# A decoder block on one core: the first block's tail goes under the expert loop, and the block input is loaded as rows and turned by TensorE

## The chip, the core and the metric

The kernel runs as one program on one core of a Trainium2 chip. The core has TensorE (PE: matmuls, with its weight loads shown as PEld), VectorE (DVE), ScalarE (ACT), GpSimd (POOL) and SyncE (SP, which here only issues DMAs), each with its own instruction stream; they meet through semaphores. Sixteen DMA engines move data between HBM and the on-chip memories. The metric is device time in microseconds (us), lower is better.

## The reference, cut to what matters

```python
h = x
xn = rmsnorm(h, norm_mix_w)                       # x: (1, 1024 tokens, 1024 channels), float32
proj = xn @ w_in                                  # q/k/v for 8 stick-breaking heads, q/k/v/o/i/f for 4 mLSTM heads, 2 gates
mixed = (sigmoid(g_sb) * (y_sb @ w_branch_sb) + sigmoid(g_ml) * (y_ml @ w_branch_ml)) @ w_out
h = h + mixed
hn = rmsnorm(h, norm_ffn_w)
q  = (hn @ w_query).reshape(T, 8 heads, 2, 128)   # PEER: product keys
s1, s2 = q[:, :, 0] @ keys1, q[:, :, 1] @ keys2   # 128 scores each; top 16 of each, then top 16 of the 256 sums
e_idx, gate = ...                                 # 8 * 16 = 128 experts of 16384 per token, softmax gates
act = gelu(expert_u[e_idx] . hn)                  # per token 128 rows of u (1024 floats) and 128 rows of v
h = h + (gate * act) @ expert_v[e_idx]
out = rmsnorm(h, norm_final_w)
```

## The kernel before, in words

**Two kinds of work.** The 1024 tokens are 8 tiles of 128 (`TT = 8`); two tiles make a block of 256 tokens (`NB = 4` blocks). The mixer, from the first norm to the PEER scores, is done block by block by a generator `mix(b)` in every engine's stream. One `yield` ends one step; the steps come in sections: `N_NORM` steps of norm, 13 of first projections (`PROJ1`, one 512 KB weight unit each), the stick-breaking attention (SBA, from `n_sba(b)`), `PROJ2`, `N_MIX`, `N_OUT`, `N_HN` (norm of h, and hn turned for the query matmuls), and `N_QRY = 19` steps: `QRY` units 0 to 15 are query matmuls; in steps 4, 8, 12 and 16 PE also does the scores of one of four head groups, and one step later (5, 9, 13, 17) ACT copies them out.

The expert work is done per tile in 64 slots (`PP = 64`), a pair of experts in each. POOL gathers one expert row of u and v for each of the 128 tokens (L885, 1 MB per gather, `rowsb<-uv,e_idx`) into a ring of 8 buffers (`RS = 8`, so four pairs); DVE forms the dot product with the normed row `hnrow` (L1479); ACT applies gelu (`gelu`, L1070), the gate (L1080) and builds two diagonal matrices (`spread`, L1085); PE adds the v rows (`add_rows`, L819), which signals `v_done`. A gather waits for the `v_done` of the pair that had its buffer. Before a tile's gathers DVE must have picked the experts: `top_parts(i, g)` for each of four head groups (36 parts per tile), then `gates`. In tile 0 (i = 0) one part is done in each slot, for groups 1 to 3 of tile 0 and all of tile 1; in later tiles the 36 parts of the next tile lie in slots 24 to 59.

**The order.** On every engine, `mix(0)` runs to its end first; SP then loads `hnrow` of tile 0 (`load_hn(0)`, L517); DVE does `top_parts(0, 0)` and `gates(0, 0, 1)` before its first dot, ACT does its half of these gates (L1065) behind step 13 of N_QRY. Then the loop over tiles and slots starts, and blocks 1 to 3 lie under it: `steps[s][b]` says how many steps of block b are done in slot s. A planner spreads each block's steps over its slots (block 1: slots 0 to 99, block 2: 100 to 227, block 3: 228 to 355) so that the estimated cost of a step (`load_of`, 2.0 for a norm step) is even over the slots. In a slot PE does first `add_rows` and then the mixer steps, except in slot 0 of a tile.

**The norm of the block input.** x comes in transposed, from a second copy of x made by the host (`xT`), as 8 loads of 128 KB in runs of 1 KB (`load_x`, L426), channels on partitions. ACT squares each chunk of 128 channels (L913), PE sums over channels with a matmul by ones (L623), two chunks at a time because `sq` has two buffers; ACT takes the square root (L916), DVE the reciprocal over 128x256 (L1131), and DVE multiplies each chunk by weight and factor (L1135, 8 times). The loads for block b+1 are issued in odd steps of block b's N_QRY. All loads but the gathers go through SP's queue, which is in order.

Of the kernel before, what the change touches and what calls it, by code (L numbers as in the profile page):

```python
# [11 lines left out]
ALU = mybir.AluOpType  # L12
# [3 lines left out]
P = 128  # L16
# [49 lines left out]
def build(nc, xT, x, vecs, w_feat, w_if, w_tok, w_merge, w_out, w_query, keysT, uv, rows, out):  # L66
    ctx = ExitStack()
    with ctx:
# [62 lines left out]
        sq = cut(A_EXT, 2 * N).rearrange("p (u t) -> p u t", u=2)  # L131
        rstd = cut(A_EXT + 2 * N, N)
# [64 lines left out]
        x_loaded = [sem(f"x_loaded{k}") for k in range(KD)]  # L197
        sq_ready, sq_summed, xn_ready = sem("sq_ready"), sem("sq_summed"), sem("xn_ready")
# [63 lines left out]
        for b in range(NB):  # L262
            put(("ss", b), 0, 0)
# [68 lines left out]
        N_NORM, N_PROJ1, N_PROJ2 = 7, len(PROJ1) + 1, len(PROJ2) + 1  # L332
# [3 lines left out]
        def load_of(b):  # L336
            unit = 8 * N * 1.67e-3 + 0.2
            cost = [2.0] * 7
# [39 lines left out]
        with nc.Block() as block:  # L378

            @block.sync  # L380
            def _(sp):
# [54 lines left out]

                def mix(b):
                    t0 = NT * b
                    if b == 0:
                        for k in range(KD):  # L440
                            load_x(0, k)
# [52 lines left out]
                    for k in range(N_QRY):  # L494
# [8 lines left out]
                        if k % 2 == 1 and k // 2 < KD and b + 1 < NB:  # L503
                            load_x(b + 1, k // 2)
# [8 lines left out]
                def load_hn(i):  # L513
                    sp.wait_ge(hn_stored[i], 16)
                    if i > 1:
                        sp.wait_ge(dot_done, (i - 1) * NSEL)
                    sp.dma_start(hnrow[:, i % 2, :], hn_dram[i * P:(i + 1) * P, :]).then_inc(hn7_loaded[i % 2], 16)  # L517

# [4 lines left out]
                for _step in mix(0):  # L523
                    pass
                load_hn(0)
                later = [mix(b) for b in range(1, NB)]
                for i in range(TT):
                    for p in range(PP):
# [9 lines left out]
                        for b in range(1, NB):  # L538
                            for _n in range(steps[i * PP + p][b]):
                                next(later[b - 1], None)  # L540
# [6 lines left out]
            def _(pe):  # L547
# [66 lines left out]
                def mix(b):  # L614
                    t0 = NT * b

                    for k in range(N_NORM):
                        if k < 4:
                            if k == 0:
                                vacant(pe, ("ss", b))  # L620
                            for c in (2 * k, 2 * k + 1):
                                pe.wait_ge(sq_ready, b * KD + c + 1)
                                pe.matmul(X[:, 0, 0:N], ones[:, :], sq[:, c % 2, :], start=c == 0,  # L623
                                          stop=c == KD - 1).then_inc(sq_summed, 1)
                        yield
                    for k in range(N_PROJ1):
                        if k == 0:
                            pe.wait_ge(xn_ready, (b + 1) * KD)
# [195 lines left out]
                for _step in mix(0):  # L824
                    pass
                later = [mix(b) for b in range(1, NB)]
                for i in range(TT):
                    for p in range(PP):
                        if p > 0:
                            add_rows(i, p)  # L830
                        for b in range(1, NB):
                            for _n in range(steps[i * PP + p][b]):
                                next(later[b - 1], None)
                        if p == 0:
                            add_rows(i, p)
# [55 lines left out]
            def _(act):  # L891
# [13 lines left out]
                def mix(b):  # L905
                    t0 = NT * b
                    for k in range(N_NORM):
                        if k < 4:
                            for c in (2 * k, 2 * k + 1):
                                act.wait_ge(x_loaded[c], 16 * (b + 1))  # L910
                                if c >= 2:
                                    act.wait_ge(sq_summed, b * KD + c - 1)
                                act.activation(sq[:, c % 2, :], xn[:, c, :], ACT.Square).then_inc(sq_ready, 1)  # L913
                        if k == 4:
                            act.wait_ge(sq_summed, (b + 1) * KD)
                            act.activation(rstd, X[:, 0, 0:N], ACT.Sqrt, scale=1.0 / D, bias=eps[:, 0:1]).then_inc(x_taken[0], 1)  # L916
# [182 lines left out]
                later = [mix(b) for b in range(1, NB)]  # L1099
                for i in range(TT):  # L1100
                    for p in range(PP):
# [4 lines left out]
                        for b in range(1, NB):  # L1106
                            for _n in range(steps[i * PP + p][b]):
                                next(later[b - 1], None)
# [7 lines left out]
            def _(dve):  # L1116
# [9 lines left out]
                def mix(b):  # L1126
                    t0 = NT * b
                    for k in range(N_NORM):
                        if k == 5:
                            emptied(dve, ("ss", b))  # L1130
                            mark(dve.reciprocal(rstd, rstd))  # L1131
                            settle()
                        if k >= 5:
                            for c in range(4 * (k - 5), 4 * (k - 5) + 4):
# [450 lines left out]
```

## Time and profile before

| | |
|---|---|
| median of 3 runs | 3449.7 us (3446.57 to 3456.82) |
| the profiled execution | 3442.75 us |
| its span (first to last instruction) | 3440.6 us |
| PE / DVE / ACT / POOL busy | 77% / 63% / 31% / 34% |
| DMA | 1280.42 MB, mean 372 GB/s |

The page cuts the span in 40 slices of 86 us. A digit is the busy share in tenths; PEclk is the TensorE clock that was granted, in tenths of full speed; DMA is the mean busy share of the 16 DMA engines:

```profile
PE   7999687898888778887887878898787555555554
DVE  2322479776456787786447698776457755775444
PEclk8999899999998999999998989999998767777777
DMA  3335798999999999999999989999999999999997
```

The first gather is issued in the fourth slice; up to there the DMA engines are a third busy, and from the sixth on they are nearly full.

### The profile page before, as it was taken

How to read it: one execution, taken by the hardware profiler on the slowest of the kernel's cores; microseconds unless marked ns; L12 is line 12 of the kernel's file. 1: busy time of each engine (PE TensorE's matmuls, PEld its weight loads, DVE VectorE, ACT ScalarE, POOL GpSimd, SP SyncE). 2: the span in 40 equal slices, each digit the busy share in tenths (PEclk: the TensorE clock that was granted, in tenths of full speed). 3: DMA queues.
4: the chain of work that ended last, by engine and by line, in shares of the span. 5: the costliest groups of instructions: out<-in, count | busy, mean ns of one | idle time of the engine just before them, and what ended most of it. 6: DMA issues, size and time to landing. Idle time of an engine off the chain costs nothing.

```text
span 3440.6 us, 40277 instructions
## 1 busy us (share of the span) xinstructions
PE 2645.8 (77%) x14496; PEld 1346.8 (39%) x14496; DVE 2151.8 (63%) x4980; ACT 1067.3 (31%) x3378; POOL 1185.5 (34%) x1049
## 2 busy tenths in 40 slices
PE   7999687898888778887887878898787555555554
PEld 5676444455354334554353334454253111111111
DVE  2322479776456787786447698776457755775444
ACT  2111234333223363332223363332222232223222
POOL 0000233334323343333333344433233434443442
PEclk8999899999998999999998989999998767777777
DMA  3335798999999999999999989999999999999997
GB/s 111 104 120 188 290 417 322 362 416 414 399 402 406 413 356 411 418 418 406 410 414 411 415 313 406 417 419 417 417 394 419 421 415 421 421 418 407 421 421 317
DMA packets 229127, 1280.42 MB, mean 372 GB/s; under 512 B 25536, under 2 KB 29632, under 8 KB 97856
## 3 DMA queue, kind: packets, MB, share of 16 engines
q0 software_dynamic: 147456, 1073.81, 76.2%
q1 hardware_dynamic: 81472, 204.04, 16.2%
q8 instruction: 115, 1.88, 0.2%
q14 instruction: 84, 0.69, 0.1%
HBM read 1260.97 MB, written 16.78 MB: 371 GB/s over the span
## 4 chain that ended last, share of the span: by engine, by line
DMA 39%; PE 35%; DVE 13%; ACT 6%; issue 5%; POOL 3%; POOLq 0%; ACTq 0%; DVEq 0%; SPq 0%
DMA rowsb<-uv,e_idx 34%; PE yacc L819 13%; PE mixp L561 9%; DVE rowsb L1479 5%; PE mixp L586 4%; DMA wt<-w_query_ 3%; POOL rowsb L885 3%; PE mixp L610 2%; PE mixp L599 2%; DVE area L1152 2%; PE mixp L573 2%; ACT diag L1085 2%; ACT wg L1080 1%; ACT area L903 1%; ACT gmt L1070 1%
## 5 line engine op out<-in xcount | busy, mean ns | idle before, releaser
L885 POOL DMA_INDIRECT rowsb<-uv,e_idx x1024 | 1180.8, 1153 | 2223.9 <-PE yacc L819 1720.5
L1479 DVE CUSTOM_DVE_ANT_0 rowsb<-rowsb,hnrow 128x1024 f32<-128x1024 f32 x1024 | 1241.3, 1224 | 853.6 <-DMA rowsb<-uv,e_idx 830.7
L819 PE MATMUL yacc<-rowsb,diag 64*64 64x512 f32 x8192 | 1226.0, 724 | 658.5 <-ACT diag L1085 639.6
L819 PEld LDWEIGHTS yacc<-rowsb,diag 64*64 64x64 f32 x8192 | 301.0, 151 | 1411.7 <-ACT diag L1085 974.7
L1070 ACT ACTIVATE gmt<-dots 128x2 f32<-128x2 f32 x512 | 104.0, 203 | 1725.5 <-DVE dots L1479 1724.7
L561 PE MATMUL mixp<-area,wt 128*128 128x256 f32 x2304 | 538.7, 389 | 16.3 <-ACT area L903 10.0
L561 PEld LDWEIGHTS mixp<-area,wt 128*128 128x128 f32 x2304 | 434.7, 193 | 154.3 <-issue 91.5
L1085 ACT ACTIVATE diag<-ident,wg 128x64 f32<-128x64 f32 x1024 | 300.3, 340 | 16.7
L586 PE MATMUL mixp<-area,wt 128*128 128x256 f32 x1024 | 247.5, 399 | 37.7 <-DMA wt<-w_query_ 36.7
L903 ACT ACTIVATE area<-mixp 128x512 f32<-128x512 f32 (+3 forms) x384 | 162.8, 467 | 361.6 <-PE mixp L561 163.2
L1080 ACT ACTIVATE wg<-gmt,gate 128x1 f32<-128x1 f32 x1024 | 245.7, 286 | 17.4
L586 PEld LDWEIGHTS mixp<-area,wt 128*128 128x128 f32 x1024 | 199.0, 199 | 108.7 <-DMA wt<-w_query_ 48.9
L610 PE MATMUL mixp<-area,wt 128*128 128x256 f32 x512 | 119.4, 389 | 6.2 <-DMA wt<-w_merge 6.2
L599 PE MATMUL mixp<-wt,area 128*128 128x512 f32 x256 | 118.2, 609 | 3.4 <-DMA wt<-w_out_ 3.4
L573 PE MATMUL mixp<-wt,area 128*128 128x512 f32 x256 | 117.5, 606 | 1.4 <-DMA wt<-w_tok 1.4
L610 PEld LDWEIGHTS mixp<-area,wt 128*128 128x128 f32 x512 | 97.2, 194 | 34.7 <-issue 15.1
L1152 DVE TENSOR_TENSOR_SCAN area<-area 128x128 f32<-128x128 f32 (+7 forms) x64 | 86.9, 1358 | 2.2
L1479 DVE DVE_READ_ACCUMULATOR2_ANT dots<- 128x1 f32 x1024 | 84.2, 82 | 0.0
L599 PEld LDWEIGHTS mixp<-wt,area 128*128 128x128 f32 x256 | 47.3, 193 | 76.3 <-issue 74.6
L573 PEld LDWEIGHTS mixp<-wt,area 128*128 128x128 f32 x256 | 47.1, 191 | 71.9 <-issue 69.5
L643 PE MATMUL mixp<-keys_sb,area 64*128 64x512 f32 (+3 forms) x192 | 52.1, 590 | 10.3 <-ACT area L903 9.1
L654 PE MATMUL mixp<-ident,area 128*128 128x128 f32 x288 | 49.1, 309 | 10.7 <-DVE area L1154 10.5
(183 smaller groups left out, 1689.2 us busy)
## 6 DMA issues: line engine op xcount, KB each, us to landing
wt<-w_merge SPq DMA_DIRECT2D x96, 512.0 KB, 8.0
wt<-w_feat SPq DMA_DIRECT2D x80, 512.0 KB, 8.1
wt<-w_query_ SPq DMA_DIRECT2D x64, 512.0 KB, 12.1
wt<-w_tok SPq DMA_DIRECT2D x32, 512.0 KB, 10.4
wt<-w_out_ SPq DMA_DIRECT2D x32, 512.0 KB, 8.5
rowsb<-uv,e_idx POOLq DMA_INDIRECT x1024, 13.1
area<-xT SPq DMA_DIRECT2D x32, 128.0 KB, 13.6
area<-x_rows SPq DMA_DIRECT2D x4, 1024.0 KB, 17.9
```

Source lines behind the costliest of these rows:

```text
L561: last = pe.matmul(X[:, bank(key), at:at + N], w[:, c * P:(c + 1) * P], src[:, c, :], start=c == 0, stop=c == KD - 1)
L573: last = pe.matmul(X[:, bank(key), :], xn[:, 2 * n + c, t * P:(t + 1) * P], w[:, c * NCH:(c + 1) * NCH], start=n == 0 and c == 0, stop=n = ...
L586: last = pe.matmul(X[:, bank(key), at:at + N], w[:, c * NCH + f * P:c * NCH + (f + 1) * P], hnT[:, 2 * m + c, :], start=m == 0 and c == 0 ...
L599: last = pe.matmul(X[:, bank(key), :], mgT[:, n, t * P:(t + 1) * P], w[:, c * NCH:(c + 1) * NCH], start=n == 0, stop=n == KD - 1)
L610: last = pe.matmul(X[:, bank(key), f * N:(f + 1) * N], w[:, at:at + P], src[:, c, :], start=c == 0, stop=c == 3)
L819: last = pe.matmul(yacc[at:at + HP, r, c * NCH:(c + 1) * NCH], diag[r * HP:(r + 1) * HP, s, :], rowsb[r * HP:(r + 1) * HP, s, D + c * NCH: ...
L885: pool.indirect_dma_start(rowsb[:, n % RS, :], None, uv, bass.IndirectOffsetOnAxis(ap=e_idx[:, i % 2, k:k + 1], axis=0)).then_inc(row_load ...
L903: act.activation(to, src, fn, **kw).then_inc(x_taken[bank(key)], 1)
L1080: act.activation(wg[:, s:s + 1], gmt[:, s:s + 1], ACT.Copy, scale=gate[:, i % 2, k:k + 1]).then_inc(wg_done, 1)
L1085: last = act.activation(diag[:, s, :], ident7[:, :], ACT.Copy, scale=wg[:, s:s + 1])
L1152: mark(dve.tensor_tensor_scan(left[:, T - m:T][:, ::-1], back, back, 1.0, ALU.mult, ALU.min))
L1479: dve.tensor_tensor_reduce(rowsb[:, s, 0:D], rowsb[:, s, 0:D], hnrow[:, i % 2, :], 1.0, 0.0, ALU.mult, ALU.add, dots[:, s:s + 1]).then_inc ...
```

## The change

1. **Tail of block 0.** All engines run `mix(0)` only up to and with step 12 of N_QRY (`N_HEAD`, all but the last 6 steps). These last 6 steps (query units 13, 14, 15, the scores of the fourth group and the copies out) are done one per slot in slots 0 to 5 of tile 0. In slot 0 of tile 0 PE does `add_rows` ahead of the mixer step. Block 1 is spread over slots 3 to 99.
2. **Gates and hnrow of tile 0.** ACT does its half of the first gates ahead of step 12 of N_QRY. SP issues `load_hn(0)` in step 3 of block 0's N_QRY.
3. **Block input.** x is loaded as rows (tokens on partitions), 2 loads of 512 KB in runs of 4 KB, in steps 7 and 9 of N_QRY, into the place of `hn`. ACT squares a tile of 128x1024 with a sum along the row, twice, and takes the square root of 2 columns; DVE takes the reciprocal of 2 columns and makes two diagonal matrices `scale1` (128x128). PE multiplies each 128x128 piece of x by the diagonal, 16 matmuls, which turns and scales it; ACT copies 8 pieces of 128x256 out with the norm weight as scale. The section has 3 steps instead of 7, with planner costs 2.0, 4.5, 2.5. Norms of blocks 1 to 3 are done in the same new way.

```diff
-            put(("ss", b), 0, 0)
+            for c in range(4):
+                put(("xt", b, c), c)
-        N_NORM, N_PROJ1, N_PROJ2 = 7, len(PROJ1) + 1, len(PROJ2) + 1
+        N_NORM, N_PROJ1, N_PROJ2 = 3, len(PROJ1) + 1, len(PROJ2) + 1
-            cost = [2.0] * 7
+            cost = [2.0, 4.5, 2.5]
+        N_HEAD = len(cost[0]) - 6
+        for s in range(6):
+            steps[s][0] = 1
         for b in range(1, NB):
-            lo = 0 if b == 1 else NT * (b - 1) * PP - PP + BLOCK_END
+            lo = 3 if b == 1 else NT * (b - 1) * PP - PP + BLOCK_END
 # SP
-                def load_x(b, k):
-                    if b > 0 and k == 0:
+                def load_x(b, t):
+                    if b > 0 and t == 0:
                         for i in range(NT * (b - 1), NT * b):
-                            sp.wait_ge(h_stored[i], 16)
-                        sp.wait_ge(hn_ready, NT * b)
-                    sp.dma_start(xn[:, k, :], xT[k * P:(k + 1) * P, b * N:(b + 1) * N]).then_inc(x_loaded[k], 16)
+                            sp.wait_ge(hn_stored[i], 16)
+                        for n in range(NT):
+                            ready(sp, ("hT", b - 1, n, 1))
+                    sp.dma_start(xr[:, t, :], x[(NT * b + t) * P:(NT * b + t + 1) * P, :]).then_inc(x_loaded[t], 16)
-                        if k % 2 == 1 and k // 2 < KD and b + 1 < NB:
-                            load_x(b + 1, k // 2)
+                        if k == 3 and b == 0:
+                            load_hn(0)
+                        if k in (7, 9) and b + 1 < NB:
+                            load_x(b + 1, (k - 7) // 2)
 # PE, norm section
-                            for c in (2 * k, 2 * k + 1):
-                                pe.wait_ge(sq_ready, b * KD + c + 1)
-                                pe.matmul(X[:, 0, 0:N], ones[:, :], sq[:, c % 2, :], start=c == 0,
-                                          stop=c == KD - 1).then_inc(sq_summed, 1)
+                        if k == 1:
+                            pe.wait_ge(scale_ready, b + 1)
+                            for c in range(4):
+                                vacant(pe, ("xt", b, c))
+                                for f in range(2):
+                                    for t in range(NT):
+                                        at = f * N + t * P
+                                        last = pe.matmul(X[:, c, at:at + P], xr[:, t, (2 * c + f) * P:(2 * c + f + 1) * P],
+                                                         scale1[:, t, :], start=True, stop=True)
+                                last.then_inc(x_done[c], 1)
 # PE, main loop (SP, ACT and DVE alike: the steps of block 0 among those of the slots)
-                for _step in mix(0):
-                    pass
-                later = [mix(b) for b in range(1, NB)]
+                later = [mix(b) for b in range(NB)]
+                for _n in range(N_HEAD):
+                    next(later[0])
                 for i in range(TT):
                     for p in range(PP):
-                        if p > 0:
+                        if p > 0 or i == 0:
                             add_rows(i, p)
 # ACT, norm section
+                        if k == 0:
+                            for t in range(NT):
+                                act.wait_ge(x_loaded[t], 16 * (b + 1))
+                                act.activation(sq[:, t, :], xr[:, t, :], ACT.Square, accum_out=ssq[:, t:t + 1]).then_inc(xsq_ready, 1)
+                            act.wait_ge(xsq_ready, NT * (b + 1))
+                            act.activation(ssq[:, NT:2 * NT], ssq[:, 0:NT], ACT.Sqrt, scale=1.0 / D,
+                                           bias=eps[:, 0:1]).then_inc(xstd_ready, 1)
+                        if k == 2:
...
+                            for c in range(KD):
+                                key = ("xt", b, c // 2)
+                                ready(act, key)
+                                ins = act.activation(xn[:, c, :], X[:, bank(key), c % 2 * N:(c % 2 + 1) * N], ACT.Copy,
+                                                     scale=vec[:, V_NORM1 + c:V_NORM1 + c + 1])
...
 # ACT, head
-                for n, _step in enumerate(mix(0)):
-                    if n == len(cost[0]) - N_QRY + 13:
+                for n in range(N_HEAD):
+                    if n == len(cost[0]) - N_QRY + 12:
                         gates(0, 0, 1)
+                    next(later[0])
 # DVE, norm section
+                            dve.wait_ge(xstd_ready, b + 1)
+                            mark(dve.reciprocal(ssq[:, 0:NT], ssq[:, NT:2 * NT]))
                             settle()
+                            for t in range(NT):
+                                last = dve.tensor_scalar(scale1[:, t, :], ident[:, :], ssq[:, t:t + 1], None, ALU.mult)
+                            last.then_inc(scale_ready, 1)
```

## Rows read from the trace of the kernel before

**Rows 1.** Busy time by stretch: span, PE, PEld, DVE, ACT, POOL, PEclk, DMA share, GB/s.

```profile
341.00:364.00 23.00, 17.64 (x84) 15.19 (x83) 0.07 (x1) 2.42 (x5) 7.70 (x8) 0.93 0.97 372
364.00:384.00 20.00, 13.21 (x67) 10.91 (x65) 0.54 (x3) 5.10 (x9) 0.00 (x0) 1.00 0.74 266
384.00:399.00 15.00, 7.06 (x28) 3.25 (x32) 10.71 (x36) 5.15 (x17) 0.00 (x0) 0.66 0.16 54
399.00:436.00 37.00, 27.73 (x170) 14.14 (x163) 29.91 (x71) 13.13 (x41) 16.29 (x14) 0.91 0.92 362
700.00:1190.00 490.00, 416.32 (x2248) 229.36 (x2246) 303.91 (x741) 152.13 (x484) 172.27 (x153) 0.93 1.01 408
1190.00:1290.00 100.00, 75.02 (x577) 35.59 (x575) 87.90 (x125) 59.46 (x180) 47.97 (x34) 0.88 0.91 360
1975.00:2065.00 90.00, 71.08 (x530) 34.20 (x534) 84.78 (x107) 60.65 (x155) 38.62 (x27) 0.85 0.83 317
```

**Rows 2.** Who waited for whom from 341 to 400 us: total, times, longest.

```profile
POOL rowsb L885 <- PE yacc L819: 47.9, 1, 47.9
DVE gs L1464 <- ACT gate L1065: 25.4, 1, 25.4
DVE rowsb L1479 <- DMA hnrow<-hn_scratch: 20.6, 1, 20.6
```

**Rows 3.** POOL in order of time: the ninth gather and the 23rd.

```profile
399.06 0.93 POOL L885 DMA_INDIRECT rowsb<-uv,e_idx  x1 [47.87 <-PE yacc L819]
436.01 1.20 POOL L885 DMA_INDIRECT rowsb<-uv,e_idx  x1 [2.33 <-PE yacc L819]
```

**Rows 4.** PE in order of time: query unit 12, its scores, one slot later on.

```profile
357.22 5.29 PE L586 MATMUL mixp<-area,wt 128*128 128x256 f32 x16 [5.36 <-DMA wt<-w_query_]
362.34 1.95 PE L805 MATMUL mixp<-area 128*128 128x128 f32 x16
422.70 1.95 PE L819 MATMUL yacc<-rowsb,diag 64*64 64x512 f32 x16
424.58 3.72 PE L561 MATMUL mixp<-area,wt 128*128 128x256 f32 x16
```

**Rows 5.** ACT in order of time: the table load of the first gates.

```profile
364.94 1.28 ACT L1065 ACT_TABLE_LOAD   x1
```

**Rows 6.** The head in order of time, ACT and PE.

```profile
5.65 1.28 ACT L913 ACT_TABLE_LOAD   x1 [5.65 <-POOL ident L875]
20.29 30.66 PE L561 MATMUL mixp<-area,wt 128*128 128x256 f32 x128 [6.26 <-DVE area L1135]
30.26 0.60 ACT L903 ACTIVATE keys_sb<-mixp 128x512 f32<-128x512 f32 x1 [15.20 <-PE mixp L561]
37.17 0.60 ACT L903 ACTIVATE keys_sb<-mixp 128x512 f32<-128x512 f32 x1 [6.31 <-PE mixp L561]
```

**Rows 7.** Two stretches of the head, columns as in rows 1.

```profile
3.00:4.00 1.00, 0.00 (x0) 0.00 (x0) 0.00 (x0) 0.00 (x0) 0.86 (x5) 1.00 0.85 258
15.00:16.00 1.00, 0.00 (x0) 0.00 (x0) 0.81 (x1) 0.06 (x1) 0.00 (x0) 0.84 0.00 0
```

**Rows 8.** The norm of h in order of time: first square, then the reciprocal.

```profile
296.33 1.06 ACT L1029 ACTIVATE area<-area 128x1024 f32<-128x1024 f32 x1 [42.54 <-DVE area L1353]
300.32 0.17 DVE L1358 RECIPROCAL ssq<-ssq 128x2 f32<-128x2 f32 x1 [2.82 <-ACT ssq L1037]
```

**Rows 9.** Groups by line and shape: busy us, mean ns.

```profile
L903 ACT ACTIVATE area<-mixp 128x256 f32<-128x256 f32 x112 | 40.9, 376 | 153.3 <-PE mixp L561 147.5 <-PE mixp L654 5.5 <-PE mixp L643 0.2
L1270 DVE TENSOR_SCALAR area<-area 128x128 f32<-128x128 f32 x24 | 6.5, 280 | 20.0 <-ACT area L1010 20.0
```

**Rows 10.** DVE in order of time: three SBA scans of block 2.

```profile
1188.12 0.28 DVE L1149 TENSOR_TENSOR area<-area,tri 128x128 f32<-128x128 f32 x1
1195.38 0.28 DVE L1149 TENSOR_TENSOR area<-area,tri 128x128 f32<-128x128 f32 x1
1200.65 0.29 DVE L1149 TENSOR_TENSOR area<-area,tri 128x128 f32<-128x128 f32 x1
```

More of the change, by code:

```diff
@@ L439, in mix @@
                     if b == 0:
-                        for k in range(KD):
-                            load_x(0, k)
+                        for t in range(NT):
+                            load_x(0, t)
                         sp.dma_start(vec[:, :], vecs).then_inc(vec_loaded, 16)
@@ L537, in _ @@
                                 load_scores(i + 1, g)
-                        for b in range(1, NB):
+                        for b in range(NB):
                             for _n in range(steps[i * PP + p][b]):
-                                next(later[b - 1], None)
+                                next(later[b], None)
                         if i + 1 < TT and p == PP - 8:
@@ L627, in mix @@
                         if k == 0:
-                            pe.wait_ge(xn_ready, (b + 1) * KD)
+                            for c in range(4):
+                                emptied(pe, ("xt", b, c))
                         if k < len(PROJ1):
@@ L822, in add_rows @@
                     last.then_inc(v_done, 2)
-                for _step in mix(0):
-                    pass
-                later = [mix(b) for b in range(1, NB)]
+                later = [mix(b) for b in range(NB)]
+                for _n in range(N_HEAD):
+                    next(later[0])
                 for i in range(TT):
                     for p in range(PP):
-                        if p > 0:
+                        if p > 0 or i == 0:
                             add_rows(i, p)
-                        for b in range(1, NB):
+                        for b in range(NB):
                             for _n in range(steps[i * PP + p][b]):
-                                next(later[b - 1], None)
-                        if p == 0:
+                                next(later[b], None)
+                        if p == 0 and i > 0:
                             add_rows(i, p)
@@ L907, in mix @@
                     for k in range(N_NORM):
[L908 to L916, printed above, removed]
+                        if k == 0:
[6 more added lines that the diff above has]
+                        if k == 2:
+                            if b > 0:
+                                for i in range(t0 - NT, t0):
+                                    act.wait_ge(h_stored[i], 16)
+                            else:
+                                act.wait_ge(vec_loaded, 16)
+                            for c in range(KD):
[3 more added lines that the diff above has]
+                                                     scale=vec[:, V_NORM1 + c:V_NORM1 + c + 1])
+                                if c % 2 == 1:
+                                    ins.then_inc(x_taken[bank(key)], 1)
                         yield
@@ L1095, in _ @@
                 act.wait_ge(io_set, 3)
-                for n, _step in enumerate(mix(0)):
-                    if n == len(cost[0]) - N_QRY + 13:
+                later = [mix(b) for b in range(NB)]
+                for n in range(N_HEAD):
+                    if n == len(cost[0]) - N_QRY + 12:
                         gates(0, 0, 1)
-                later = [mix(b) for b in range(1, NB)]
+                    next(later[0])
                 for i in range(TT):
@@ L1105, in _ @@
                             norm(i - 1)
-                        for b in range(1, NB):
+                        for b in range(NB):
                             for _n in range(steps[i * PP + p][b]):
-                                next(later[b - 1], None)
+                                next(later[b], None)
                         if i == 0 and p in GATES_AT:
@@ L1501, in _ @@
                 dve.wait_ge(vec_loaded, 16)
-                for _step in mix(0):
-                    pass
-                later = [mix(b) for b in range(1, NB)]
+                later = [mix(b) for b in range(NB)]
+                for _n in range(N_HEAD):
+                    next(later[0])
                 for _part in top_parts(0, 0):
@@ L1522, in _ @@
                             final_norm(i - 1)
-                        for b in range(1, NB):
+                        for b in range(NB):
                             for _n in range(steps[i * PP + p][b]):
-                                next(later[b - 1], None)
+                                next(later[b], None)
                     for _part in parts:
```

32 lines of the change are left out of this document (12 added, 20 removed).

## The prediction

> **What bounds the kernel now.** I read the strips of the page first: the DMA engines are nearly full from the sixth slice to the end and a third busy up to the fourth. The table of stretches says it in numbers: from 700 to 1190 us their share is 1.01 at 408 GB/s, so whatever bytes are left set the time. It also shows where they are not full: 384 to 399 us (0.16), 364 to 384 (0.74), and two later stretches, 1190 to 1290 (0.91) and 1975 to 2065 (0.83), where DVE is busy 88 and 94% of the time [rows 1]. So the time is the head, in which DMA can't be the limit, plus the bytes at some 410 GB/s, plus the holes. A change pays where it shortens the head or fills a hole.
>
> The waits between 341 and 400 us name the first hole. POOL issued its first 8 gathers from 341 and then stood 47.9 us until PE had added the first pair. DVE stood 25.4 us for ACT's half of the gates and then 20.6 us for hnrow [rows 2]. The ninth gather left at 399.06 [rows 3]. The order in time gives the reason: ACT's table load for the gates came at 364.94 [rows 5], because that call stood behind the copy of the third group's scores, which PE did at 362.34 after unit 12 had waited 5.4 us for its weights [rows 4]; and hnrow was the last load that SP issued before the loop.
>
> **Part 1: tail, gates, hnrow.** Times here are those of the old trace; the head's own gain comes after. The experts of group 0 are known at 341 either way. ACT now does the gates there: its table load and exponential end at about 343, DVE's three small steps by 344. hnrow is loaded some 60 us sooner, in a stretch where SP's queue has little ahead of it: hidden. The first dots then wait for rows 0 and 1 of the gathers, which share 372 GB/s with the weights [rows 1], so land near 350. ACT's gelu stands behind its copy of the third query group at 352 and gives the first diagonals at 356. PE is late next: its stream has unit 12 (357.22) and the scores (362.34) ahead, so add_rows of pair 0 runs from 364.3 to 366.3 and gather 9 leaves at 366.6, not 399.06: 32 us sooner.
>
> This lead shrinks, since slots 0 to 5 now carry the moved steps. A slot with one unit costs PE 1.95 + 3.72 = 5.7 us [rows 4]. The x loads now put 0.5 MB where 0.13 MB stood before the weights of units 13 and 14; at 372 GB/s that is 1 us of waiting, and I count it. Pair 1 ends at 373.5, pair 2 at 379.6, pair 3 at 385.2. The fourth group's scores (1.95) follow, and the norm of block 1 in slots 3 to 5. Pair 4 waits in ACT's stream for two squares, a root and two table loads: 393. The 16 turning matmuls cost 3.9 (below): pair 5 ends at 399. The 8 copies (376 ns each [rows 9]) hold unit 0 of block 1 to 400.5: pair 6 at 406. Pair 7 ends at 411.6, with the 1 us 412.6. Its buffer frees the 23rd gather. Before, that one left at 436.01 [rows 3]: 23.4 us sooner. One unit of block 1 is then still to do that was done before, 0.52 MB or 1.3 us of DMA. That leaves 22.
>
> A second count, by DMA time alone: from 341 to 436 the engines stood 23 x 0.03 + 20 x 0.26 + 15 x 0.84 + 37 x 0.08 = 21.5 us [rows 1]. If DMA is what binds on both sides, no more can be won there. I take 21. Bounds: 18, if the pace of pairs leaves DMA 15% idle over the 25 us from 366; 25, if PE and DVE bind instead and the lead of the 23rd gather is kept and a little more.
>
> **Part 2: the norm of block 0 in the head.** Before, the first projection started at 20.29. Its 8 units took 30.66 us, though two units take 37.17 - 30.26 = 6.91: 3.0 us were lost, because the clock had fallen (0.84 in 15 to 16 us, PE having stood since 14) [rows 6, 7]. Now: ACT starts at 5.65 and has its table at 6.93. x is there: 1 MB from 2 us on at 258 GB/s lands at 6 [rows 7], and the second tile isn't needed before 8. The norm of h has just this sequence, two squares, table load, root: from the first square to the reciprocal 300.32 - 296.33 = 3.99 us [rows 8]. So reciprocal at 10.9, then two diagonals of 280 ns [rows 9], PE from 11.8. Eight fp32 matmuls of 128 columns take 1.95 us [rows 4], 16 take 3.9: 15.7. ACT copies behind PE, the last two add 0.75, handovers 0.3: the projection starts at 16.8. PE never stands over 1 us between, so the 3.0 us aren't lost either: 20.3 + 3.0 - 16.8 = 6.5. The other end: the turning at the low clock (7.8 us) and the loss in the units as before: 20.3 - 20.7 = -0.4. I take 5. Compute sets the pace up to 341, weights come in time there, so this passes on whole.
>
> The row shows the granted clock at 1.00 from 3 to 4 us, with no matmul yet run [rows 7]. The Trainium skill (TensorE: Matmul & The Clock Gate, part 1) says otherwise: "the default state is throttled, and activity releases the throttle". By the row the gain is 6.5; by the rule the 16 matmuls start at 1.2 GHz, some 2 us of it go, and the rest of the sum stands.
>
> **Part 3: the norms of blocks 1 to 3.** DVE loses a 128x256 reciprocal and 8 products for each block, ACT gains some 2 us, PE 1. All this lies under transfers that fill DMA to 1.01 [rows 1], so nothing, unless the cover is gone: at most 2 us either way. The loads move 3.1 MB in runs of 4 KB instead of 1 KB. The early stretch, which holds only the 1 KB runs, shows 258 GB/s at share 0.85, 304 for a full share [rows 7]; the middle shows 404 [rows 1]. 10.4 - 7.8 = 2.6 us at most, none at least; I take 1.
>
> **Part 4: what the planner does.** The norm section costs 9 instead of 14 in its estimate, with 3 steps instead of 7. I worked the slots out from `load_of`: the SBA scans of block 2 begin in slot 117 instead of 119, of block 3 in 245 instead of 247. Those are slots in which DVE still has parts of `top_parts` (24 to 59 of the tile, to slots 123 and 251). Two scans one slot apart with parts are 1195.38 - 1188.12 = 7.3 us apart, without 1200.65 - 1195.38 = 5.3 [rows 10]; two gathers need 5.2 us of DMA. So two more such slots open the hole by 2 x 2.1 = 4 us in block 2, in block 3, whose hole is 15 us against 9 [rows 1], by 7. That is 11 as the bad end. The ring of four pairs hides a lag of about one slot, and the stretch without parts gets shorter. I take a loss of 3; the good end is a gain of 2. Block 1 moves one slot later, where parts lie in every slot: nothing.
>
> **Sum.** 21 + 5 + 1 - 3 = 24 us. Against the profiled execution, 3442.75 (span 3440.6), that is 3418.8. The median of the runs shown is 7 us above that execution; 3449.7 - 24 gives 3426.
>
> **Rivals.** (a) Most of it is given back in the DVE holes: lead 18, head 1, scans -9, loads 0: a gain of 10, 3440. For it: the holes exist and DVE is nearly full in them. Against: before, three scans overlapped and the hole was 9 us in all, tile change included. (b) The change doesn't do what it says: the first pairs come sooner, but block 1 is squeezed into 97 slots and ACT, PE and DVE wait for each other in slots 3 to 8, so the loop is where it was by slot 20; only some of the head's gain stays: 3447. Against: POOL's 47.9 us are one wait with one cause. (c) Slower: PE's clock falls in the new slots 0 to 8. PE sets the pace there; if it stands between units as it did from 14 us on, a slot costs 11.3 instead of 5.7 us. Eight such slots cost 45 us, the net is 21 slower: 3471. It decides from the fourth such slot (24 / 5.7). Against: from 364 to 384, with two waits for weights in it, the clock stayed at 1.00 [rows 1].
>
> **How the numbers follow.** Forecast 0.73, (a) 0.15, (b) 0.08, (c) 0.04. About 0.3%, 10 us, can be told from no change. Rival (a) lies on that bound, and mostly falls to faster. Faster 0.85, same 0.10, slower 0.05. All good ends together are 36 us, 3413, and 5 more for the spread of the runs: 3408. The high end takes in rival (a): 3441.
>
> **What would show it.** First projection at 17 us, with the clock at 1.00 up to 26. Ninth gather near 362 (366.6 less 5), with POOL's longest wait for PE at 13 to 17 us instead of 47.9; DVE's waits for gates and hnrow gone; the 23rd gather at 407 to 410; DMA share from 384 to 399 above 0.8. Holes of about 12 and 20 us at blocks 2 and 3. I am wrong if gather 9 leaves after 375, if the clock is at half between slots 0 and 8, or if the 23rd gather is 25 us sooner and the end isn't.

## The result, and the profile after

| | before | after |
|---|---|---|
| median | 3446.57 us (3438.97 to 3456.82, 5 runs) | 3417.57 us (3413.49 to 3419.48, 5 runs) |
| profiled execution | 3442.75 | 3417.57 |
| its span | 3440.6 | 3415.4 |

The ratio is 0.9914, 95% interval 0.9892 to 0.9935: 22 to 37 us faster by the runs, 29.0 by the two medians, 25.2 by the two profiled executions. The forecast was 24 us.

The stretches that answer to [rows 1], same columns (span, PE, PEld, DVE, ACT, POOL, PEclk, DMA share, GB/s), after:

```profile
341.00:364.00 23.00, 17.36 (x73) 14.59 (x72) 9.68 (x33) 5.41 (x11) 8.67 (x8) 0.85 0.98 381
364.00:384.00 20.00, 17.00 (x95) 10.66 (x94) 9.47 (x26) 4.79 (x17) 5.50 (x5) 0.91 1.01 408
384.00:399.00 15.00, 11.36 (x67) 6.45 (x66) 7.90 (x24) 9.41 (x21) 3.81 (x5) 0.80 0.95 363
399.00:416.00 17.00, 17.00 (x110) 11.32 (x110) 11.06 (x24) 7.43 (x24) 6.43 (x6) 0.98 0.85 309
```

DVE works in the first of them (9.68 us instead of 0.07): the first dots. The DMA engines are full where they stood at 0.74 and 0.16. The waits from 341 to 400, against [rows 2]:

```profile
POOL rowsb L896 <- PE yacc L830: 36.4, 5, 15.2
DVE rowsb L1501 <- DMA rowsb<-uv,e_idx: 19.6, 10, 3.3
PE mixp L593 <- DMA wt<-w_query_: 8.6, 2, 5.6
...
DVE gs L1486 <- ACT gate L1087: 2.6, 1, 2.6
```

POOL's one wait of 47.9 us has become five of 36.4 us in all, the longest 15.2. The wait for hnrow is gone, the wait for the gates is 2.6 us instead of 25.4, and DVE waits for gathered rows, as it does in the rest of the kernel. POOL in order of time: the first, ninth, 13th and 23rd gather [rows 3].

```profile
340.50 1.14 POOL L896 DMA_INDIRECT rowsb<-uv,e_idx  x1 [334.92 <-DVE gate_raw L1477]
...
367.03 0.94 POOL L896 DMA_INDIRECT rowsb<-uv,e_idx  x1 [15.23 <-PE yacc L830]
...
382.85 0.94 POOL L896 DMA_INDIRECT rowsb<-uv,e_idx  x1 [8.11 <-PE yacc L830]
...
415.52 0.94 POOL L896 DMA_INDIRECT rowsb<-uv,e_idx  x1 [3.35 <-PE yacc L830]
```

Gathers are a good ruler, since both kernels do the same 1024 in the same order. This is by how much the changed kernel's n-th gather leaves sooner than before (its lead), from POOL's rows of the two traces:

```
gather        1     9    13    23    25    65   129   193   257   289   449   513   705  1024
lead, us    0.9  32.0  22.7  20.5  20.5  19.7  21.7  23.8  22.4  22.3  27.7  21.6  23.5  24.7
```

So 0.9 us come from the head, 19.6 from the stretch between the first and the 25th gather, 4.2 from all that follows, and 0.5 from the last pair.

**The head.** PE and ACT in order of time, after:

```profile
11.70 6.54 PE L632 MATMUL mixp<-area 128*128 128x128 f32 x32 [11.70 <-DVE area L1157]
19.48 2.83 PE L568 MATMUL mixp<-area,wt 128*128 128x256 f32 x12 [1.24 <-ACT area L935]
```

```profile
26.66 0.60 ACT L914 ACTIVATE keys_sb<-mixp 128x512 f32<-128x512 f32 x1 [7.54 <-PE mixp L568]
33.56 0.60 ACT L914 ACTIVATE keys_sb<-mixp 128x512 f32<-128x512 f32 x1 [6.31 <-PE mixp L568]
```

PE starts at 11.70, as worked out (11.8), but the 16 turning matmuls take 6.54 us, not 3.9; the projection starts at 19.48, not 16.8. The units then run at full speed: the first two are done 3.6 us sooner than in [rows 6]. At the first gather 0.9 of these 3.6 us are left.

### The profile page after: what moved, and what is told of

It reads as the page before. It is cut to its first block, busy times and chain, and to the rows that moved or that the text cites. A ratio compares the mean times of both kernels' runs of the same rounds, so it can differ in the third digit from the quotient of the medians.

```text
span 3415.4 us, 40366 instructions
## 1 busy us (share of the span) xinstructions
PE 2640.8 (77%) x14560; PEld 1350.9 (40%) x14560; DVE 2137.6 (63%) x4956; ACT 1077.5 (32%) x3394; POOL 1191.2 (35%) x1049
## 4 chain that ended last, share of the span: by engine, by line
DMA 38%; PE 36%; DVE 11%; ACT 6%; issue 5%; POOL 3%; POOLq 0%; ACTq 0%; DVEq 0%
DMA rowsb<-uv,e_idx 35%; PE yacc L830 14%; PE mixp L568 9%; DVE rowsb L1501 5%; PE mixp L593 3%; POOL rowsb L896 3%; PE mixp L606 2%; DMA wt<-w_query_ 2%; PE mixp L580 2%; PE mixp L617 2%; ACT diag L1107 2%; DVE area L1174 2%; ACT wg L1102 2%; DMA wt<-w_out_ 1%; DVE area L1205 1%
## 5 line engine op out<-in xcount | busy, mean ns | idle before, releaser
L1102 ACT ACTIVATE wg<-gmt,gate 128x1 f32<-128x1 f32 x1024 | 245.5, 286 | 17.4
## 6 DMA issues: line engine op xcount, KB each, us to landing
wt<-w_tok SPq DMA_DIRECT2D x32, 512.0 KB, 10.8
```

The source lines that it names most:

```text
L1102: act.activation(wg[:, s:s + 1], gmt[:, s:s + 1], ACT.Copy, scale=gate[:, i % 2, k:k + 1]).then_inc(wg_done, 1)
```

## The experiments

Each was timed in five rounds beside the kernel before, whose medians in the three sets were 3447.96, 3449.86 and 3448.47 us. Ratios are to it.

**The parts alone.** `e1_norm_only` is the changed kernel with `N_HEAD = len(cost[0])`, no tail steps, block 1 from slot 0, gates and hnrow as before.

> Part 3 of the change alone (x as rows, new norm); block 0 runs to its end before the loop, gates and hnrow come late as before. My theory: the norm is worth little by itself: the first gather leaves 1 to 5 us sooner, the ninth 1 to 5 us sooner, and in slots 0 to 4, where the old norm let ACT and PE wait for each other, 2 to 4 us more; in all 3 to 8 us faster than before. Rival: in the changed kernel the lead over before was only 0.9 us at the first gather and 25 at the end, so the norm gives only that 0.9: the same as before within 2 us, and the ninth gather at 398.

`e2_tail_only` is the kernel before with tail, gates and hnrow:

```diff
+        N_HEAD = len(cost[0]) - 6
+        for s in range(6):
+            steps[s][0] = 1
-            lo = 0 if b == 1 else ...
+            lo = 3 if b == 1 else ...
+                        if k == 3 and b == 0:
+                            load_hn(0)
...
-                    if n == len(cost[0]) - N_QRY + 13:
+                    if n == len(cost[0]) - N_QRY + 12:
                         gates(0, 0, 1)
...
```

> Parts 1 and 2 alone (six last steps in slots 0 to 5, gates and hnrow sooner) with the old norm and the transposed x. My theory: ninth gather at 366 to 368 as in the changed kernel, 23rd gather 16 to 20 us sooner than before (the old norm in slots 3 to 6 costs 2 to 4 us), 17 to 22 us faster than before. Rival: tail and norm only pay together, since the old norm stalls ACT and PE in slots that now also carry the tail: under 12 us.

`e3_gates_hnrow_only` keeps of these only the two early issues; `mix(0)` runs to its end first.

> The kernel before with only the gates and the load of hnrow issued sooner; block 0 runs to its end before the loop. My theory: DVE's two waits (25.4 and 20.6 us) go, but PE and ACT have block 0's steps 13 to 18 first, so the first diagonals come at 386 and the ninth gather at about 391 to 393 instead of 399: 5 to 8 us faster. Rival: hnrow was the whole reason of the 47.9 us wait, then the ninth gather leaves before 375 and it is 20 us faster.

`e4_tail_gates_hnrow_late` is the opposite, the tail without the early issues:

```diff
-                        if k == 3 and b == 0:
-                            load_hn(0)
                 for _n in range(N_HEAD):
                     next(later[0])
+                load_hn(0)          # SP
...
+                gates(0, 0, 1)      # ACT
```

> The changed kernel with ACT's gates behind step 12 and hnrow loaded only after SP's step 12. My theory: hnrow is issued at 364 and lands 12 to 17 us later behind gathers and weights, so pair 0 is added at about 380 and the ninth gather leaves at 380 to 384 instead of 367; 10 to 14 us slower than the changed kernel. Rival: the DMA engines are full from 341 to 384 in the changed kernel, so what starts later there is only put off and the end moves by under 4 us.

| | median us | ratio, 95% interval | 9th gather | lead at 25th | lead at last |
|---|---|---|---|---|---|
| changed kernel | 3417.57 | 0.9914 (0.9892 to 0.9935) | 367.0 | 20.5 | 24.7 |
| e1 norm only | 3433.18 | 0.9954 (0.9936 to 0.9971) | 398.0 | -1.4 | 10.8 |
| e2 tail, gates, hnrow | 3424.58 | 0.9935 (0.9918 to 0.9952) | 366.9 | 22.0 | 21.8 |
| e3 gates, hnrow | 3441.75 | 0.9982 (0.9970 to 0.9994) | 393.5 | 3.5 | -8.8 |
| e4 tail, late gates and hnrow | 3429.62 | 0.9945 (0.9926 to 0.9964) | 379.8 | 12.2 | 13.2 |

The tail with its two early issues is the main part: e2 has the ninth gather where the changed kernel has it, and 22 us by the ratio. Neither half does it alone. e3 removes the wait for hnrow and leaves 2.6 us of the one for the gates, but POOL still stands 40 us, because PE and ACT have block 0's last steps first:

```profile
393.53 0.94 POOL L886 DMA_INDIRECT rowsb<-uv,e_idx  x1 [40.01 <-PE yacc L820]
```

(The profiled execution of e3, 3451.19, is the slowest of its twelve, so its lead at the end says less than the median.) e4 has PE free, but the old wait for hnrow is back, 21.0 us long, and the DMA engines stand again (share 0.38 from 364 to 384). Its waits from 330 to 400, then that stretch:

```profile
POOL rowsb L895 <- PE yacc L829: 42.1, 4, 32.8
...
DVE rowsb L1499 <- DMA hnrow<-hn_scratch: 21.0, 1, 21.0
```

```profile
364.00:384.00 20.00, 8.22 (x36) 4.35 (x40) 12.04 (x39) 4.79 (x17) 2.70 (x2) 0.59 0.38 136
```

e3 and e4 came out as my theory had them, e2 a little above it. The norm alone was expected at 3 to 8 us and gave 15 by the median, 10 to 22 by the interval, against both theories. Its trace is 7.1 us behind at the 65th gather, 11.5 ahead at the 193rd and 10.8 at the last. The two parts don't add up to the whole: e1 and e2 are 16 and 22 us by their ratios, the changed kernel 30, so on top of the tail the norm brings some 7 us, and the intervals of e2 and the changed kernel overlap. Two experiments below look for the reason.

**The head.** `e6_warm_start` lets PE work before x is normed:

```diff
                 pe.wait_ge(consts_set, N_CONST)
+                for _n in range(18):
+                    pe.matmul(X[:, 0, 0:P], ones[:, :], tri[:, :], start=True, stop=True)
```

> The changed kernel with 18 matmuls of 128 columns on constants at the start of PE's stream, before x is normed; their result is overwritten. My theory: the 16 turning matmuls took 6.5 us instead of 3.9 because the clock really was low, whatever the record says; with PE at work from 5.7 us they take 4 to 4.5, and the first projection starts at 17.0 to 17.5 instead of 19.48. Rival: they are slow for another reason (ACT's copies out, weights read from the 1024-wide tile): no change, 19.5. What reaches the first gather is 0 to 5 us either way, since a shift of the head moves the places where the clock is low later on; the time is the changed kernel's within 4 us.

3416.40 us, 0.9899 (0.9884 to 0.9914): the time of the changed kernel. PE in order of time:

```profile
5.00 5.68 PE L557 MATMUL mixp<-tri,ones 128*128 128x128 f32 x36 [5.00 <-POOL mcol L882]
11.61 3.84 PE L634 MATMUL mixp<-area 128*128 128x128 f32 x32 [0.93 <-DVE area L1159]
16.69 13.62 PE L570 MATMUL mixp<-area,wt 128*128 128x256 f32 x62 [1.24 <-ACT area L937]
```

The same 16 matmuls take 3.84 us and the projection starts at 16.69. So the low clock was the cause, though the table of the changed kernel shows a granted clock of 1.00 all through its 6.54 us: its first clock record begins only at 17.4 us, and the table counts what lies before as full. The first two units end 6.4 us sooner than in [rows 6]. Yet at the first gather the lead is 3.5.

The rest goes in places where the clock falls later in the head. By ACT's copies, matched one by one, the changed kernel's lead is 3.6 us at 27 us, 4.3 at 97, 2.6 at 145 and 0.9 at 320. One unit of the mixer in the changed kernel, and the same unit in `e12` (below):

```profile
139.90 5.31 PE L568 MATMUL mixp<-area,wt 128*128 128x256 f32 x16
```

```profile
139.54 3.62 PE L568 MATMUL mixp<-area,wt 128*128 128x256 f32 x16
```

And the stretch around it, PE busy and granted clock only, for the changed kernel and then `e12`:

```profile
136.00:146.00 10.00, 8.06 (x26) 0.83 0.24 79
```

```profile
136.00:146.00 10.00, 8.06 (x35) 1.00 0.35 113
```

PE is busy 8.06 of 10 us in both, but at the lower clock only 26 matmul records fit in, not 35. The instructions up to there and PE's stop of 1.38 us just before are the same; the clock is 0.83 in one and 1.00 in the other. A second such place lies at 286 to 310 us (0.79 in the changed kernel, 0.86 in e12 and in the kernel before). The first costs 1.7 us on that unit; over the second the lead falls from 2.6 to 0.9.

How much of the head's gain is left differs from execution to execution. The first gather left at 336.7 to 340.8 us in the eleven kernels with the new norm, 338.6 on the mean, and at 341.4, 340.2 and 342.2 in the three with the old one. In the ten without warm start the turning is the same code and took 5.16 to 6.71 us. The three where it took longest (6.54 in the changed kernel, 6.68 in e1, 6.71 in e5) are also the three in which the clock falls at 140 us, and their first gathers are the last, at 340.5 to 340.8; those of the other seven leave at 336.7 to 339.7. What decides where the clock falls isn't shown.

**Is sooner always better?** `e7_tail_of_7` moves one step more, the unit whose weights come late:

```diff
-        N_HEAD = len(cost[0]) - 6
-        for s in range(6):
+        N_HEAD = len(cost[0]) - 7
+        for s in range(7):
-            lo = 3 if b == 1 else ...
+            lo = 4 if b == 1 else ...
```

> The changed kernel with seven steps in the tail, not six: unit 12 of the query matmuls, which waits 5.6 us for its weights, is now behind the adding of pair 0; block 1 starts in slot 4. My theory: the first diagonals are there at 355, so pair 0 is added at 355 to 357 and the ninth gather leaves at 357 to 358 instead of 367.0; but the DMA engines were at 0.98 to 1.01 from 340 to 384 already, so of these 10 us only 0 to 4 reach the 23rd gather and the end. Rival: the ring runs dry in that stretch and all 10 us are won: 3408.

3416.24 us, 0.9905 (0.9891 to 0.9919): no change. The ninth gather leaves at 351.6, 15.5 us before that of the changed kernel (10 were expected), and the 25th at 414.9, 6.1 sooner, of which 3.4 are its head. Stretches of e7:

```profile
340.00:364.00 24.00, 17.92 (x103) 13.15 (x102) 11.29 (x38) 6.69 (x20) 10.71 (x10) 0.99 1.01 401
364.00:384.00 20.00, 15.06 (x65) 9.72 (x65) 11.41 (x32) 2.54 (x10) 2.86 (x4) 0.76 1.02 417
```

The transfers were full already, at 0.98 and 1.01 in the changed kernel. The gathers issued sooner only stand in line, and by the 129th gather the lead is 22.3, against 21.7.

`e8_x_loads_sooner` issues the two loads of x in steps 3 and 5 (`if k in (3, 5)`).

> The changed kernel with the two loads of x in steps 3 and 5 of N_QRY instead of 7 and 9. My theory: in block 0 these 1 MB then pass while the DMA engines are half idle (share 0.46 from 303 to 336), the weights of units 12 to 14 come 1 to 3 us sooner, and that reaches the ninth and the 23rd gather: 1 to 3 us faster than the changed kernel. Rival: the weights wait for the gathers and not for x, and nothing changes.

3413.72 us, 0.9897 (0.9882 to 0.9911). At the 25th gather it is 5.0 us ahead of the changed kernel, at the last 1.5, and 1.3 of either is head. What it wins in the first slots isn't kept. Its median is 3.9 us below that of the changed kernel, with intervals that overlap, so its theory and its rival stay undecided.

**What the new norm is worth in the loop.** `e9_runs_of_1kb` loads x as rows, but in pieces of 128 KB and runs of 1 KB:

```diff
-                    sp.dma_start(xr[:, t, :], x[...rows of tile...]).then_inc(x_loaded[t], 16)
+                    for q in range(4):
+                        sp.dma_start(xr[:, t, q * N:(q + 1) * N], x[...rows..., q * N:(q + 1) * N]).then_inc(x_loaded[t], 16)
```

> The changed kernel with x still loaded as rows, but each tile of 512 KB in 4 loads of 128 KB, in runs of 1 KB as before the change. Theory A: the short runs are what the old loads cost: then this is slower than the changed kernel by what the two stretches with old loads lost in the traces, 4 to 5 us for each block of 1 to 3 that loads one (gathers 288 to 448: 498 us where the new norm has 493.5), 5 to 12 us in all. Theory B, my prediction's bound from the shares: at most 2.6 us, then it is within 3 us of the changed kernel, and the gain of the new norm comes from the engines.

3420.93 us, 0.9922 (0.9910 to 0.9935); gathers 289 to 449 take 492.0 us against 493.3. Theory A placed 4 to 5 us in this stretch, and falls by it; the time alone, 3.4 us above the changed kernel by the medians with overlapping intervals, would not decide (the profiled execution, 3416.08, is the fastest of its six). That 1 KB runs cost nothing isn't shown. At 3 to 4 us only runs of 1 KB pass in e9, as in the kernel before [rows 7], and only runs of 4 KB in the changed kernel. First e9, then the changed kernel:

```profile
3.00:4.00 1.00, 0.00 (x0) 0.00 (x0) 0.00 (x0) 0.00 (x0) 0.86 (x5) 1.00 0.80 245
```

```profile
3.00:4.00 1.00, 0.00 (x0) 0.00 (x0) 0.00 (x0) 0.00 (x0) 0.86 (x5) 1.00 1.00 389
```

For a full share that is 306 against 389 GB/s, by which the 1 MB of x in the stretch would cost 0.7 us more (an estimate from these two rows): less than the 492 to 495.5 us over which the kernels with the same slots spread.

`e10_dve_work_back` puts back on DVE what the new norm took off:

```diff
+                            if b > 0:
+                                rec = sq[:, 1, 3 * N:4 * N]
+                                mark(dve.reciprocal(rec, rec))
+                                settle()
+                                for c in range(7):
+                                    own = sq[:, c // 4, c % 4 * N:(c % 4 + 1) * N]
+                                    mark(dve.scalar_tensor_tensor(own, own, vec[...], rec, ALU.mult, ALU.mult))
```

> The changed kernel with a 128x256 reciprocal and 7 products on DVE put back into the norm step of blocks 1 to 3, on scratch that nothing reads: 4.7 us of DVE for each block, 14 in all, about what the new norm took off DVE. Theory A: transfers cover it, no change within 2 us of the changed kernel. Theory B: DVE is the near-full engine around slots 88 to 123 and 216 to 251, and the norm alone won 15 us mainly because DVE was relieved: 8 to 14 us slower than the changed kernel.

3413.61 us, 0.9903 (0.9887 to 0.9920): 14 us of DVE work cost nothing that shows. Theory B falls.

**The planner's slots.** `e5_old_slots` sets the costs of the norm steps to 2, 7, 5:

> The changed kernel with planner costs 2, 7, 5 for the three norm steps, 14 in all as before, so that all later steps of blocks 2 and 3 lie in the slots that they had before (scans from slots 119 and 247, not 117 and 245). My prediction's part 4: the two slots cost 3 us (between a gain of 2 and a loss of 11), so this is 3 us faster than the changed kernel, with a hole at block 2 of 9 us and not 11. Rival: in the trace of the changed kernel the lead over before stays at 22 to 24 us through both holes, so the shift costs nothing: within 2 us of the changed kernel, 3417.

`e12_old_slots_b2_b3` does so for blocks 2 and 3 only:

> The changed kernel with planner costs 2, 7, 5 for blocks 2 and 3 only; block 1 keeps 2, 4.5, 2.5. It tells apart where the 6.7 us of the kernel with old slots came from. If from the scans of block 2 that no longer overlap (gathers 192 to 288 took 297 us on the mean in six kernels with new slots, 292 in four with old ones): 4 to 6 us faster than the changed kernel, 3412, with the lead over before at the 25th gather still 20.5 us. If from block 1's first slots (lead of 29.7 us at the 25th gather instead of 20.5): the same as the changed kernel, 3417.

`e11_tail7_x_slots` joins e5, e7 and e8:

> Three of the single changes together: tail of seven steps (block 1 from slot 4), x loads in steps 3 and 5, planner costs 2, 7, 5. If they add up, from 6.7, 3.9 and 1.3 us of the medians: 12 us faster than the changed kernel, 3406. Rival: tail and early x loads fill the same transfers around 340 to 400, and their lead was gone by gather 256 in both traces, so only the planner's part stays: 3409 to 3412.

| | median us | ratio, 95% interval | lead at 1st | at 25th | at last gather |
|---|---|---|---|---|---|
| e5 | 3410.88 | 0.9885 (0.9869 to 0.9902) | 0.6 | 29.7 | 31.9 |
| e12 | 3416.23 | 0.9908 (0.9893 to 0.9923) | 4.7 | 29.5 | 31.2 |
| e11 | 3418.51 | 0.9906 (0.9891 to 0.9922) | 3.8 | 35.1 | 23.3 |

The intervals of all three overlap that of the changed kernel; e5's median is 6.7 us below it, e12's, with the same slots in blocks 2 and 3, only 1.3. So no version is shown to beat the changed kernel, and the three don't add up: e11's median misses both of its expectations. e12 has the time that its second theory said, but not the lead: block 1 has the slots of the changed kernel, and yet the lead at the 25th gather is 9.0 us larger, 3.8 of it head. Most of the other 5.2 are unit 14, here in the changed kernel and then in e12:

```profile
375.26 5.41 PE L593 MATMUL mixp<-area,wt 128*128 128x256 f32 x16 [3.00 <-DMA wt<-w_query_]
```

```profile
369.16 3.72 PE L593 MATMUL mixp<-area,wt 128*128 128x256 f32 x16
```

It waits for nothing in e12 and runs at full clock, though the code up to there is the same. So such a lead is no proof of anything in block 1. In e5 it isn't like for like either: by the DMA records 27.0 MB were moved from its first to its 25th gather, 30.4 in the kernel before. At the level of stretches the traces say more. Time from gather to gather, us, mean and range over the profiled executions, by where the scans of block 2 begin:

```
gathers                   193 to 289               289 to 449               449 to 545
slot 117 (8 kernels)      297.0 (293.4 to 300.6)   493.3 (492.0 to 495.5)   301.2 (296.7 to 305.8)
slot 119 (6 kernels)      291.3 (287.3 to 294.0)   497.5 (495.3 to 500.1)   300.2 (297.9 to 301.7)
```

With the new slots the stretch at block 2 takes 5.7 us more, and the next gives 4.2 back. These are times, not holes. The DMA records of the same fourteen traces tell how long the engines stood (the stretch less the time that packets took, as a mean over the 16 engines) and what was moved:

```
gathers                   193 to 289         449 to 545          193 to 545
slot 117, stood, MB       8.2 us, 116.2      17.2 us, 113.9      16.6 us, 435.7
slot 119, stood, MB       6.8 us, 114.3      12.6 us, 115.9      13.4 us, 435.7
```

At block 2 the hole is only 1.4 us deeper, and 1.9 MB more pass in it; at block 3 it is 4.6 us deeper, which the time doesn't show because 2.0 MB less pass. Over all three stretches the bytes are equal, the time is 2.6 us longer and the engines stand 3.2 us more. The second column goes by the slots and not by the norm: e5, e11 and e12, with the new norm, stand at 495.3 to 498.0 with the three old-norm kernels; e9 with short runs and e10 with DVE's work stand at 492.0 and 492.8.

## Why the prediction was right

**What bounds the kernel.** As read. DMA at 1.01 before and after, and the experiments that issued more, sooner, into a full stretch (e7, e8, and e11 with other slots) gained nothing at the end that the intervals show.

**The total owes something to luck.** Of 24 us, 19.6 + 0.9 + 4.2 + 0.5 were measured for 21 + 5 - 2: the head fell short by 4.1, and the loop with its last pair gave 4.7 where parts 3 and 4 said a loss of 2. These two errors nearly cancel; the mechanism of part 1 is what carries the result.

**Part 1, 21 us predicted, 19.6 measured.** The chain was right in its links: the ninth gather was said for 366.6 in old time and left at 367.0, which is 367.9 in old time; the wait for hnrow is gone and 2.6 us are left of the one for the gates; PE is late next, through unit 12's weights. The 23rd gather left at 415.5 where 412.6 less 5 for the head was said. Of these 8 us, 4.1 are the head. The rest is in unit 14, which waited 3.0 us for its weights and then took 5.41 us at the low clock, where I had 1 us for both units, 13 and 14. The second count, DMA's standing time, gave 21.5 and was nearer than the chain of instructions, which gave 23.4. It is no ceiling, though: in e6 and e12, with the same code in this stretch, the 25th gather leaves 18.0 and 24.8 us sooner beyond the head. In the changed kernel the engines stand 1.2 us in the three stretches up to 399; a new hole of 2.6 us lies at 399 to 416, behind the norm of block 1. That the early issues and the tail are both needed is shown by e3 and e4. Early gates and early hnrow were not tried apart; the wait that comes back in e4 is that for hnrow.

**Part 2, 5 us predicted, 0.9 measured.** This is the term that was off. The start of PE was right to 0.1 us. What failed is the clock: I gave the row weight that showed 1.00 before any matmul, and took only part of the loss. The Trainium skill (TensorE: Matmul & The Clock Gate, part 1) says that PE starts throttled. The durations agree with it, 6.54 us cold and 3.84 after other work, and the row was wrong. With the clock up the sum itself comes out: 6.5 us said, 6.4 at the first two units of e6. The second failure is "this passes on whole": a lead isn't kept in the head, and 3.4 us of a lead that had grown to 4.3 went in two places where the clock fell. Between the means of the eleven kernels with the new norm and the three with the old one the term is 2.7 us, so the changed kernel's 0.9 is at its low end.

**Parts 3 and 4, -2 predicted, +4.2 measured.** The planner's shift cost in all what I took, 2.6 us and 3.2 us of standing engines, against my 3. By blocks it isn't what was worked out: the hole at block 2 grew by 1.4 us (4 predicted at worst), at block 3 by 4.6 (7 at worst). The loads of x in runs of 4 KB instead of 1 KB: at most 2.6 predicted, nothing to be seen in e9's trace. DVE's relief, predicted nothing, is nothing in e10. So of the norm's own gain in the loop, 10 to 22 us less the head when it stands alone, none of the causes tried accounts. The DMA records say where it lies. From the first to the last gather the kernel before moved 1231.8 MB in 3034.7 us of an engine's time and the engines stood 33.3 us; the changed kernel 1230.6 MB in 3026.2 us, standing 18.0; e1 1231.0 MB in 3026.7 us, standing 31.1. So 15 of the changed kernel's 24 us are standing time and 8 or 9 are packets that took less time, and e1's 10 are nearly all of the second kind. But e2, with the old norm, has 3027.8 us too, so it isn't the norm alone. The runs of one kernel spread over 4 to 18 us, and gathers 25 to 289 alone took 850 to 868 us in the fourteen profiled executions, so a few us in the loop can't be placed by single traces. What the norm gives there stays open.

**Rivals.** (a) would have shown a smaller lead at the end than at the 25th gather; it is larger. (b) is excluded by the ruler: the lead at the 65th gather is 19.7. (c): the clock did fall in slots 1 and 4 (0.60 from 376 to 380, 0.61 and 0.54 from 392 to 400), each time beside a wait of PE of 3.0 and 3.6 us: two slots, not the four from which it decides, and it rose again each time. A clock at half between slots 0 and 8 was one of my signs of being wrong, so that sign was drawn too tight.

## What to carry to other kernels

When a ring of buffers stands on one long wait, write down for each engine what is queued ahead of the first use, and move all of it together: here the early issues were worth 6 us alone, without them the changed kernel lost 12, and tail and early issues gave 22 together. Then size the gain by the time that the bounding resource really stands in that stretch (21.5 us here, 18.0 to 24.8 measured); past that point, issuing sooner bought nothing (15 us at the ninth gather, 0 at the end). Compare stretches by standing time and bytes as well as by time, since a fixed stretch can hold other bytes. For a small edit in a pipelined loop, time the same numbered transfer in both traces instead of the two ends, and don't believe a head's gain before it has passed the places where TensorE's clock can fall.

## What the runs showed of the hardware that was not expected

- The granted clock of a stretch reads 1.00 ahead of the trace's first clock record, also where matmuls run slowly: 16 matmuls of 128 columns took 6.54 us under "1.00" (first record at 17.4 us), 3.84 us when PE had worked since 5.0 us.
- The same instructions behind the same stop of 1.38 us got a clock of 0.83 from 136 to 146 us in one execution and 1.00 in another, with a start 0.4 us apart. A unit of 8 matmuls took 5.31 or 3.62 us.
- At the start of the kernel the DMA engines moved 389 GB/s where only 4 KB runs passed and 245 where only 1 KB runs did (3 to 4 us, changed kernel and e9); in a stretch where the DMA engines are full the split showed no cost (492.0 against 493.3 us for 160 gathers, one trace each).
